# Second block's recurrence as in-place products of gates, with projections laid between its levels, and a new order at the start of the attention heads

## The reference, cut to what matters

```python
# attention of the first block: 8 heads, two score maps each, blockwise causal mask
p = softmax(where(allowed, q_blk @ k.T * scale, -inf)); p = p[:, :, 0] - lam * p[:, :, 1]
o = p @ v                                     # then rms_norm per head, and @ w_o

# second block: p = h @ w_in, in seven pieces of 512 columns
log f, k = log_sigmoid(p_f), sigmoid(-p_f)    # forward and backward gates (pieces 0, 1)
v = p[2]; q = silu(p[3]) * 128 ** -0.5; gate = silu(p[4]); u = gelu(p[5]); vv = gelu(p[6])
b = cumsum(log f)                             # within a chunk
scores[t, s] = sum_k q[t, k] * k[s, k] * exp(b[t, k] - b[s, k])   # s <= t
o = scores @ v + (q * exp(b)) @ state         # forward, and the same flipped in time
o = rmsnorm(o_f + o_b) * gate
o_mlp = u * (w_spatial @ layernorm(vv) + b_spatial)
x = x + g1 * (concat([o, o_mlp]) @ w_out)
```

## Time and profile before

| | |
|---|---|
| median of 3 runs | 1422.3 us (1419.84 to 1424.62) |
| the profiled execution | 1420.42 us |
| its span, first to last instruction | 1418.6 us |
| mean granted TensorE clock | 0.944 of full speed |
| PE (matmul) busy | 1255.7 us, 89% |
| DVE (VectorE) busy | 964.1 us, 68% |
| ACT (ScalarE) busy | 662.8 us, 47% |
| POOL (GpSimd) busy | 253.7 us, 18% |
| read from HBM | 197.75 MB, 140 GB/s over the span |

### The profile page before, as it was taken

The page is one execution under the profiler, slowest core; times in us unless marked ns, Lnnn a source line. Parts: engine busy times, 40 slices in busy tenths (PEclk is TensorE's granted clock), DMA queues, the critical chain, the costliest instruction groups (busy, mean ns, idle before and its releaser), DMA issues.

```text
span 1418.6 us, 21943 instructions
## 1 busy us (share of the span) xinstructions
PE 1255.7 (89%) x9218; PEld 1167.3 (82%) x9218; DVE 964.1 (68%) x1300; ACT 662.8 (47%) x855; POOL 253.7 (18%) x171
## 2 busy tenths in 40 slices
PE   3998988987899999799688889999788958999995
PEld 3887877775899999696468888999778948999995
DVE  6767667445478874646664666864569964999994
ACT  4564344124544345555475564444464543554442
POOL 0000000000354441000000111110016501344431
PEclk9999999798999999899799999999899979999997
DMA  7440001000677654353133677875342303445530
GB/s 269 149 149 31 30 1 61 1 1 31 226 255 257 242 179 149 107 190 119 34 112 123 207 268 271 297 252 176 121 147 90 119 0 119 162 169 185 189 130 30
DMA packets 122656, 200.20 MB, mean 141 GB/s; under 512 B 3264, under 2 KB 111168, under 8 KB 112320
## 3 DMA queue, kind: packets, MB, share of 16 engines
q1 hardware_dynamic: 117664, 168.05, 35.0%
q0 software_dynamic: 3456, 25.17, 4.7%
q10 hardware_dynamic: 1440, 5.60, 1.1%
HBM read 197.75 MB, written 1.05 MB: 140 GB/s over the span
## 4 chain that ended last, share of the span: by engine, by line
PE 59%; DVE 29%; ACT 6%; issue 4%; DMA 0%; DVEq 0%; POOL 0%; ACTq 0%
PE bank L611 12%; PE bank L612 11%; PE bank L613 11%; DVE buf L2367 7%; DVE ring_r L1694 7%; PE bank L694 3%; PE bank L696 3%; PE bank L695 3%; PE bank L627 2%; ACT high L1133 2%; DVE work L1950 2%; PE bank L837 2%; PE bank L849 2%; DVE work L1946 2%; DVE buf L2272 1%
## 5 line engine op out<-in xcount | busy, mean ns | idle before, releaser
L611 PE MATMUL bank<-part,high 128*128 128x256 f32 x1664 | 484.2, 291 | 59.5 <-DVE part L1701 54.4
L612 PE MATMUL bank<-part,high 128*128 128x256 f32 x1664 | 480.3, 289 | 0.0
L613 PE MATMUL bank<-part,ring_r 128*128 128x256 f32 x1664 | 479.8, 288 | 0.0
L1694 DVE TENSOR_TENSOR ring_r<-ring,high 128x2048 fp32r<-128x2048 f32 (+1 forms) x155 | 343.6, 2226 | 194.6 <-ACT high L1133 192.2
L611 PEld LDWEIGHTS bank<-part,high 128*128 128x128 f32 x1664 | 329.4, 198 | 66.2 <-issue 46.8
L612 PEld LDWEIGHTS bank<-part,high 128*128 128x128 f32 x1664 | 329.4, 198 | 0.8 <-issue 0.8
L613 PEld LDWEIGHTS bank<-part,ring_r 128*128 128x128 f32 x1664 | 329.2, 198 | 0.0
L1133 ACT ACTIVATE high<-ring 128x2048 fp32r<-128x2048 f32 x155 | 295.0, 1905 | 31.7 <-PE bank L613 21.4
L1606 POOL TENSOR_TENSOR ring_r<-ring,high 128x512 fp32r<-128x512 f32 x44 | 92.8, 2109 | 537.1 <-ACT high L1133 537.0
L694 PE MATMUL bank<-part,high 128*128 128x256 f32 x528 | 151.9, 288 | 9.2 <-POOL part L1600 4.9
L695 PE MATMUL bank<-part,high 128*128 128x256 f32 x528 | 150.6, 285 | 0.0
(11 more groups left out here) (277 smaller groups left out, 1719.2 us busy)
## 6 DMA issues: line engine op xcount, KB each, us to landing
ring<-in_wide SPq DMA_DIRECT2D x122, 1024.0 KB, 5.9
ring<-in_down SPq DMA_DIRECT2D x33, 1024.0 KB, 4.9
buf<-in_wide POOLq DMA_DIRECT2D x24, 1024.0 KB, 7.0
con<-in_cons SPq DMA_DIRECT2D x1, 1472.0 KB, 11.0
ring<-in_wide SPq DMA_DIRECT2D x2, 576.0 KB, 7.1
buf<-in_wide ACTq DMA_DIRECT2D x1, 1024.0 KB, 5.1
buf<-in_wide SPq DMA_DIRECT2D x1, 1024.0 KB, 5.2
buf<-in_ctx_t ACTq DMA_DIRECT2D x1, 1024.0 KB, 4.7
```

The costliest lines, as they stand in the source:

```text
L611: mm(bank, ah, bh, start=start, stop=False, skip_group_check=shared)
L612: mm(bank, ah, bl, start=False, stop=False, skip_group_check=shared)
L613: return mm(bank, al, bh, start=False, stop=stop, skip_group_check=shared)
L1694: v.tensor_tensor(low, raw, hi.bitcast(F32), ALU.subtract).then_inc(sem("unit_low"), 1)
```

## The change

**Recurrence.** The sums of logs, their exponentials and the buffers `wgt`, `pre_t` and `suf_t` go. `reach_q` starts as q times the gate f, `reach_k` as 1 - f, each for both directions (8 heads' rows). After each level the far half of each block pair in `reach_q` is multiplied by the decay of the near block, and the near half of `reach_k` by that of the far block, in place (`reach_on`: four products of 128x512). The decay of whole blocks is kept apart, and each level's is the product of pairs of the level before (`block_decays`, 1024 columns, then 512, 256 and so on). GpSimd has no part in it. The gates come straight out of PSUM through two sigmoids, f and 1 - f. TensorE's `level` takes `reach_k` and `reach_q` as its two operands in place of one buffer twice.

**Order of the mixer.** The pieces of `in` are streamed as q, forward gate, backward gate, vv, u, v, output gate. Six units run first, then `diag`, then each level is followed by one unit (`BETWEEN`). The statistics of vv, its norm and the spatial gate's product and output move to levels 2, 4 and 5. The rows of `w_out` are rolled by half, so that the spatial half of the mix comes first: `mo_half(i, 0)` of three units runs before or between `go` and `gsum`, and the other halves behind.

**Attention.** VectorE turns only queries 0 and 1 before it takes the maxima of heads 0 and 1; queries 2 and 3 and one weight unit's low part come behind. TensorE computes the first two context pieces before `turn_probs(0)`. Three of the four `sum_heads` and `root_heads` are done together, after head 6 and head 7. `scale_heads` and `low_piece` all move to the end of the loop. Rope and token banks come from smaller sets.

```diff
-CTX_TAKEN = (0, 2, 3, 5, 6, 8, 9, 10, 11)
+CTX_TAKEN = (2, 3, 4, 6, 7, 8, 9, 10, 11)
+SUMS_AT = 6
-IN_ORDER = (0, 1, 3, 2, 4, 5, 6)
-IN_TOKENS = (3, 6)
+IN_ORDER = (3, 0, 1, 6, 5, 2, 4)
+IN_TOKENS = (3, 5)
+BETWEEN = {0: (3, 0), 1: (3, 1), 2: (4, 0), 3: (4, 1), 4: (5, 0), 5: (5, 1), 6: (6, 0)}
+Z_AFTER = 5
+MO_SPLIT = 3
...
# bank plan
-        for n in ("akrot", "aqrot"):
+        for n, among in (("akrot", (0, 1, 2, 3)), ("aqrot", (6, 7, 4, 5))):
...
-        plan_tokens("av", 1, [("av", 2), ("av", 3)])
+        plan_tokens("av", 1, [("av", 2), ("av", 3)], (2, 3))
...
# TensorE, attention
+                context(CTX_PIECES[:CTX_TAKEN[0]])
                 for h in range(HEADS):
                     turn_probs(h)
...
-                    if h % 2 and h >= 3:
-                        sum_heads((h - 3) // 2)
+                    if h == SUMS_AT:
+                        for j in range(3):
+                            sum_heads(j)
...
# TensorE, mixer
-                                z = wgt[l % 2][:, 4 * dr + h, t * P:(t + 1) * P]
-                                last = mm(bank[:, h * P:(h + 1) * P], z, z, start=True, stop=True)
+                                sides = [z[:, 4 * dr + h, t * P:(t + 1) * P] for z in (reach_k, reach_q)]
+                                last = mm(bank[:, h * P:(h + 1) * P], *sides, start=True, stop=True)
...
+                for l in range(LEV):
+                    level(l)
+                    if l == Z_AFTER:
+                        gate_spatial()
+                    if l in BETWEEN:
+                        in_half(*BETWEEN[l])
...
+                in_half(6, 1)
+                mo_half(0, 0)
...
+                for i in range(1, MO_SPLIT):
+                    mo_half(i, 0)
...
+                for i in range(MO_SPLIT):
+                    mo_half(i, 1)
+                mo_half(3, 0)
+                mo_half(3, 1)
...
# ScalarE, mixer
+                        if d == 0:
+                            release(act_(piece(q_x, j), bank_of(key)[:, :], ACT.Silu), key)
+                        else:
+                            at = 2 * (d - 1) + j
+                            own.go(act_(piece(f_x, at), bank_of(key)[:, :], ACT.Sigmoid))
+                            release(act_(piece(reach_k, at), bank_of(key)[:, :], ACT.Sigmoid, scale=-1.0), key)
                         ahead("in", d, j)
...
# GpSimd
-                for l in range(LEV + 1):
...
-                    own.step(add(sl, sl, pr[:, :, b - 1:b].to_broadcast([P, n, b]), ALU.add))
...
# VectorE, attention
-                for j in range(4):
-                    rope_queries(j)
-                ahead("av", 1, 1)
+                rope_queries(0)
+                rope_queries(1)
...
                 attend_scores(0)
                 attend_scores(1)
+                ahead("av", 1, 1)
+                rope_queries(2)
                 for h in range(HEADS):
                     attend_probs(h)
+                    if h == 0:
+                        rope_queries(3)
+                        ahead("ctx", 0, 0)
...
# VectorE, mixer
+                    ins = v.scalar_tensor_tensor(reach_q[:, four, :], q_x, HG_SCALE, f_x[:, four, :], ALU.mult, ALU.mult)
...
+                        own.go(v.tensor_tensor(q_far, q_far, decay[:, :, near:near + 1].to_broadcast([P, n, b]), ALU.mult))
+                        if both:
+                            own.go(v.tensor_tensor(k_near, k_near, decay[:, :, far:far + 1].to_broadcast([P, n, b]), ALU.mult))
...
+                for l in range(LEV):
...
+                    reach_on(l)
+                    own.settle()
+                    eng.sem_inc(sem("reach_ready"), 1)
+                    if l + 2 <= LEV:
+                        block_decays(l + 1)
+                    take_scores(l)
+                    if l == 2:
+                        values_stats()
+                    if l == 4:
+                        values_normed()
+                    if l == Z_AFTER:
+                        spatial_out()
+                    ahead("in", *BETWEEN[l])
```

More of the change, by code:

```diff
@@ L231, in plan_proj, with plan_tokens @@
                     unit_job(name, c, j, (name, 2 * c + j))
-        def plan_tokens(stage, c, keys):
+        def plan_tokens(stage, c, keys, among=tuple(range(NBANK))):
             for key in keys:
-                place(key)
+                place(key, among)
             unit_mid(stage, c, 0)
@@ L1491, in _ @@
                 parts("hx")
-                def in_out(d, dst):
+                for d in range(3):
                     for j in range(2):
@@ L2227, in _ @@
                 down_ahead(1)
[L2228 removed]
+                for half in range(2):
+                    ahead("in", 0, half)
+                for d in (1, 2):
+                    ahead("in", d, 0)
                     for j in range(2):
[L2230 to L2235 removed]
@@ L2245, in _ @@
[L2245 to L2253 removed]
+                        wait_freed(eng, ("in", 0, j))
@@ new lines, in values_normed @@
+                def values_normed():
+                    eng.wait_ge(sem("vv_root"), 1)
+                    own.step(v.reciprocal(bna[:, :, 1:2], bna[:, :, 1:2]))
+                    for i in range(8):
+                        z = vv4[:, i // 4, i % 4, :]
+                        own.go(v.tensor_scalar(z, z, bna[:, i, 0:1], bna[:, i, 1:2], ALU.subtract, ALU.mult))
+                    own.settle()
+                    eng.wait_ge(sem("rows_in"), 16)
+                    own.step(v.tensor_tensor(vv_x, vv_x, spread(prow("sgu_g"), [P, TT, 512]), ALU.mult))
+                    v.tensor_tensor(vv_x, vv_x, spread(prow("sgu_b"), [P, TT, 512]), ALU.add).then_inc(sem("vv_ready"), 1)
@@ L2293, in _ @@
+                for d in range(2):
+                    wait_full(eng, ("cross", d))
+                reach_on(LEV, False)
+                own.settle()
+                eng.sem_inc(sem("reach_all"), 1)
+                low_piece("mix", 0)
+                low_piece("mix", 1)
                 for d in range(2):
```

391 lines of the change are left out of this document (172 added, 219 removed).

## The result

The changed kernel takes 1402.96 us (median of 4 runs, 1401.76 to 1411.57) against 1422.32 for the kernel before: a ratio of 0.9877, 95% interval 0.9835 to 0.992, or 19.4 us less. The profiled execution took 1402.62 us.

The account below looks back on a forecast made before the run. VectorE was taken to bound the mixer's levels (busy 89.4 of 92 us), TensorE its first projections. Mixer 12.9 plus attention 3.1 made 16.0 us of gain, so 1406 us in terms of the median; own range 1399 to 1412, with rivals 1395 to 1416.

Parts of the forecast that it names:

- Steps 1 and 2: Mixer's start: six units end at 1044.6, TensorE idles 3.7 us, `diag` starts at 1048.3, level 0 ends at 1055.5.
- Step 3: Mixer's levels 1 to 4: 9.4 us each on TensorE, VectorE's 8.1 us round hidden, products at 0.62 us, end at 1098.8.
- Step 4: Spatial gate at level 5: TensorE idles 4.2 us, product 3.6 us at the lower clock, level 6 and its unit end at 1126.0.
- Step 5: `cross`, `go`, `gsum` and projection halves to 1150.6, then an uncovered root chain of 7.3 us; TensorE starts again at 1157.4.
- Step 6: Mixer's end: upper halves of the output projection, with VectorE and ScalarE rounds of 5.2 to 5.8 us; norm ends at 1181.2.
- Attention: Attention stage: first turn at 682.8, last low piece 5.5 us sooner, 2.4 us lost to the lower clock; gain 3.1 us.
- the upper bound: Most that attention's heads could gain: 1.4 from the first turn, 5.6 from context pieces, 2.3 from a split, 9.3 us.
- (a): Rival: more comes through, as the clock recovers faster and the mixer's tail overlaps; mixer 18, attention 8, 1396 us; chance 0.17.
- (b): Rival: level products in place cost what the old ones did; 1415 us at 1.25 each, 1436 at 2.01; chance 0.07.
- (c): Rival: attention gives nothing or costs 3 us, its roots at the end exposed in full; 1409 to 1412 us; chance 0.08.
- (d): Rival: spatial norm and splits fall behind, TensorE waits at levels for low parts; two waits of 4 us, 1414; chance 0.06.

Follow-up runs that it names:

- pool_adds: The changed kernel with 48 GpSimd additions of 128 x 512 into unused space beside the levels; 1430.83 us, ratio 1.0063 to the kernel before.
- gsum_early: The changed kernel with the sums of squares issued ahead of the two split halves of the output projection, and the first half behind `go`; 1396.85 us.
- tail: The changed kernel with the weight splits, but for one unit, moved from between the residual's additions at the mixer's end to the feed-forward network; 1402.36 us.
- mixer_start: The changed kernel with only the front of its attention part: the heads' sums, roots, scales and splits stay spread over the loop; 1401.70 us.
- double_products: The changed kernel with four extra VectorE additions of 128 x 512 in each of seven levels, GpSimd idle; 1409.92 us.

## Why the prediction was right

The forecast was 1406, and 1403 was measured: 16 us of gain predicted, 19.4 measured in the medians and 18.2 in the spans. Part of the closeness is luck, since errors of opposite sign cancel: the attention gave 2.7 us more than predicted, the mixer 1.3 less, and the third feed-forward network gave 0.8 where nothing was predicted (not traced further). Put on the clock of the trace before (the mixer's start moved from 1001.33 to 1007.13, so 5.80 is added to every time), its steps stand like this.

**Steps 1 and 2.** The sixth unit ends at 1044.5 (predicted 1044.6) and `diag` starts at 1048.15 after 3.68 idle (1048.3 after 3.7). `diag` and level 0 take 8.4 us, not 7.2: the lower clock lasted through all of `diag` (3.79 us for sixteen matmuls) and about a third of level 0 (4.79 for 3.73). Level 1 starts at 1061.8 (1061.2).

**Step 3.** Price of a product, 0.62: right, 0.60 from one to the next. Rounds of 9.0 to 9.3 for 9.4, no gap. Level 5 starts at 1098.6 (1098.8). The table load and root at level 3 were hidden, as worked out.

**Step 4.** 4.39 idle (4.2), z at 1106.8 (1106.7) and cold (3.78 for 3.6). Level 6 and its unit end at 1126.1 (1126.0).

**Step 5.** `gsum` ends at 1150.9 (1150.6), TensorE starts again at 1157.6 (1157.4). `gsum` itself took 1.88 for 0.9: it is four matmuls of 512 columns, which I had priced as eight of 128 instead of sixteen; that neighbouring groups overlap by some 0.16 us each (`go` starts at 1130.59, ahead of the half's end at 1130.75) made up for it.

**Step 6.** From there to the norm's end 24.8 us, predicted 23.8. The ping-pong of VectorE and ScalarE is what the chain of waits shows, in the rounds worked out (5.6, 5.1, 5.0 us between additions). Two terms were too small: the first addition comes 5.5 us after TensorE's restart, not 5.1, and the norm's last four matmuls run at the lower clock after an idle of 2.93 us and take 2.08. I had priced the end from the last addition at 2.5; it took 3.7. With the rounds 0.5 us shorter in sum, that is nearly all of the difference between 12.9 predicted and 11.6 measured.

**Attention.** This is where the size was off: 3.1 predicted, 5.8 measured (6.3 if one counts from the attention layer's first matmul). The first turn at 683.26 (682.8) and the clock's penalty of 2.5 us (2.4) were right, and so was "some 4 us" of idle. The heads gained more than the upper bound: the last turn came at 731.85 for 740.87 before, 9.0 us sooner, or 9.5 with the 0.5 by which this execution entered the stage later. Of the upper bound of 9.3 I then took off 3.8 for the roots collected at the end ("the last low piece at about 754.5 ... a gain of 5.5"). In the trace they cost 1.1 us between the last turn and the last low part. In the kernel before a root chain stood there too, and the last low part was used 19.2 us after the last turn (20.3 now), so most of the new chain replaced one that was exposed already. The prediction looked at the new chain's 6.3 us and not at what it stood in for.

**Rivals.** (a) asked for a mixer of 18 and an attention of 8: neither. Against it the prediction said that the new idle stretches are longer than those after which the clock fell; in the trace before it had fallen after idles from about 2 to 12.3 us, so that was a loose reading, but the clock did stand at 0.50 behind all four. (b) did not happen, and `pool_adds` shows that it would have been worse than priced. (c) and (d) did not happen; (d)'s waits for low parts at the levels are in no row. The chances named for "faster" add up to 0.93, not 0.92.

## What to carry to other kernels

Price a VectorE instruction by who works beside it: a product took 1.75 us beside GpSimd's additions and 0.68 a few us later without them, and decays, splits and the norm got dearer with it, not only the instructions under discussion. Look at single instructions beside the other engine's rows, since a group's mean mixes both prices. When an idle of 4 us or more is left on TensorE, price it twice, once for itself and once for the 2 us of lower clock behind it (21.51 us for 18.97 behind 4.18 us, 17.2 for 14.9 behind 6.68); a shorter one may or may not bring the second price, as the section below shows. Look for independent matmuls that are issued just ahead of such a hole: in `gsum_early`, putting the short step that starts a chain ahead of the long independent ones cost 1.4 us of waiting ahead of `go` and paid 8.1. When work is collected at the end of a stage, compare the exposed chain with the one that was exposed before, and when work is moved out of a chain, look for who waits for it next (`tail`).

## What the runs showed of the hardware that I had not expected

TensorE's clock can drop in a stretch where nothing was changed, in one execution and not in the next (1.00 or 0.50 at 312 to 318 us), though TensorE had been busy 5.41 and 5.55 of the 6 us ahead of it. It put the profiled execution of `mixer_start` 7.3 us behind that of the changed kernel before the changed part began, more than most of the edits that were to be compared. The length of an idle did not decide alone whether the clock fell behind it. The norm's last four matmuls come after 2.93 us of idle in both kernels: they took 2.08 us in the changed kernel and 1.13 in `double_products`, where a level behind 3.41 us of idle ran at full speed too (3.84 us, granted clock 1.00). In the changed kernel's attention, an idle of 2.31 us at 710.98 left the clock at 1.00, and one of 2.32 us at 723.43 was followed by 0.55 over the next 3.5 us. Behind the idles of 3.68 us and more of that trace it stood at 0.50 each time. And a VectorE TENSOR_SCALAR of 128 x 128, with one tensor operand, took up to 1.42 us for 0.33 while GpSimd was adding.
